# adaLN weight loads moved between the layers of a diffusion backbone step, and the place of one combine in the expert groups

## The reference

```python
mod = (silu(cond) @ ada_w[i] + ada_b[i])            # 1024 -> 6 * 1024, per sequence
sh1, sc1, g1, sh2, sc2, g2 = split(mod, 6)
h = rms_norm(x, norm1_g[i]) * (1 + sc1) + sh1
m = (pool_mix, attention, fourier_mix)[i % 3](h)    # layers 0, 1, 2, 3: pool, attention, fourier, pool
x = x + g1 * m
h = rms_norm(x, norm2_g[i]) * (1 + sc2) + sh2
x = x + g2 * moe(h)                                 # 16 experts of width 512, top 2 in the best group of 4
```

## Time and profile before

| | us |
|---|---|
| median of 3 runs (lowest, highest) | 1356.53 (1354.65, 1357.44) |
| the profiled execution | 1354.35 |
| its span, first to last instruction | 1352.5 |
| TensorE busy | 1267.3 (94%) |
| VectorE busy | 391.5 |
| ScalarE busy | 328.6 |
| read from memory | 532.26 MB, 395 GB/s over the span |

### The profile page before, as it was taken

One profiled execution on the slowest core, in us unless ns is written; L12 is line 12 of the kernel. 1 busy time (PEld: TensorE's weight loads), 2 busy tenths in 40 slices (PEclk: granted clock), 3 DMA queues, 4 the chain that ended last, 5 costly groups with the idle time before them and its releaser, 6 DMA issues.

```text
span 1352.5 us, 18262 instructions
## 1 busy us (share of the span) xinstructions
PE 1267.3 (94%) x6665; PEld 576.3 (43%) x6665; DVE 391.5 (29%) x873; ACT 328.6 (24%) x692; POOL 39.3 (3%) x77
## 2 busy tenths in 40 slices
PE   3877999999999998999999999999999999999996
PEld 0433344343657544443433464443434354434342
DVE  1241222132233314222231413321322443213224
ACT  1231122121322223221221323221212452212122
POOL 3010000000000001000000000000000000000000
PEclk9878999999999999999999999999999999999999
DMA  9999999999997899899999998899999999999995
GB/s 374 419 418 421 420 422 421 423 421 421 343 381 310 324 413 402 340 412 420 421 422 422 418 377 326 339 398 420 422 422 422 415 421 363 405 422 421 421 422 227
DMA packets 87260, 535.21 MB, mean 396 GB/s; under 512 B 11192, under 2 KB 13336, under 8 KB 25760
## 3 DMA queue, kind: packets, MB, share of 16 engines
q1 hardware_dynamic: 82336, 527.47, 95.6%
q0 software_dynamic: 3120, 5.23, 1.2%
q10 hardware_dynamic: 1744, 1.73, 0.4%
HBM read 532.26 MB, written 2.12 MB: 395 GB/s over the span
## 4 chain that ended last, share of the span: by engine, by line
PE 84%; DMA 9%; DVE 4%; ACT 2%; issue 1%; SPq 0%; DVEq 0%; ACTq 0%
PE ps L1869 32%; PE ps L1915 15%; DMA ring<-in_ada_w_dram 5%; PE ps L1855 5%; PE ps L1927 5%; PE ps L1535 4%; PE ps L1499 4%; PE ps L1396 4%; PE ps L1898 3%; PE ps L1544 2%; DMA xh<-in_moe_w_up_dram 2%; DMA ring<-in_attn_wqkv_dram 2%; PE ps L1471 1%; PE ps L1886 1%; PE ps L1705 1%
## 5 line engine op out<-in xcount | busy, mean ns | idle before, releaser
L1869 PE MATMUL ps<-ring,xg 128*64 128x512 f32 x992 | 454.2, 601 | 19.6 <-ACT gu L841 12.3
L1871 PE MATMUL ps<-ring,xg 128*64 128x512 f32 x992 | 451.4, 598 | 0.0
L1869 PEld LDWEIGHTS ps<-ring,xg 128*64 128x64 f32 x992 | 127.6, 137 | 275.2 <-issue 248.2
L1915 PE MATMUL ps<-ring,gb 128*64 128x512 f32 x992 | 225.4, 595 | 0.0
L1319 DVE SCALAR_TENSOR_TENSOR gb<-ps,gslot,g2x 128x512 f32<-128x512 f32 x128 | 90.2, 746 | 257.1 <-PE ps L1915 257.1
L1871 PEld LDWEIGHTS ps<-ring,xg 128*64 128x64 f32 x992 | 126.9, 136 | 0.0
L1915 PEld LDWEIGHTS ps<-ring,gb 128*64 128x64 f32 x992 | 68.4, 137 | 132.2 <-issue 124.6
L854 ACT ACTIVATE y_hi<-gb 128x512 fp32r<-128x512 f32 x128 | 77.1, 626 | 168.3 <-PE ps L1927 108.4
L1396 PE MATMUL ps<-ring,cact 128*32 128x512 f32 x768 | 92.9, 617 | 10.3 <-ACT cact L638 5.3
L841 ACT ACTIVATE gu<-ps 128x512 f32<-128x512 f32 x64 | 38.3, 598 | 231.8 <-PE ps L1871 231.8
L1328 DVE TENSOR_TENSOR y_lo<-gb,y_hi 128x512 fp32r<-128x512 f32 x128 | 83.5, 688 | 12.5 <-ACT y_hi L854 11.9
(11 more groups left out here) (211 smaller groups left out, 1092.8 us busy)
## 6 DMA issues: line engine op xcount, KB each, us to landing
ring<-in_moe_w_up_dram SPq DMA_DIRECT2D x124, 1024.0 KB, 14.8
ring<-in_moe_w_gate_dram SPq DMA_DIRECT2D x124, 1024.0 KB, 13.6
ring<-in_moe_w_down_dram SPq DMA_DIRECT2D x124, 1024.0 KB, 15.4
ring<-in_ada_w_dram SPq DMA_DIRECT2D x96, 1024.0 KB, 17.8
ring<-in_attn_wqkv_dram SPq DMA_DIRECT2D x12, 1024.0 KB, 19.9
spare<-in_moe_w_gate_dram SPq DMA_DIRECT2D x4, 1024.0 KB, 18.8
xh<-in_moe_w_up_dram SPq DMA_DIRECT2D x4, 1024.0 KB, 12.5
hT<-in_moe_w_down_dram SPq DMA_DIRECT2D x4, 1024.0 KB, 13.8
```

The source lines that it names most:

```text
L1869: mg = pe.matmul(ps[0:SLOTS, B_GU, :], xg[:, b, e, :], wg[:, i * F:(i + 1) * F], start=(b == 0), stop=(b == DB - 1))
L1871: mu = pe.matmul(ps[SLOTS:P, B_GU, :], xg[:, b, e, :], wu[:, i * F:(i + 1) * F], start=(b == 0), stop=(b == DB - 1))
L1915: mm = pe.matmul(ps[r * SLOTS:(r + 1) * SLOTS, DOWN_BANKS[e % 2], :], acts[:, e % ACTS, j, :], w[:, i * D + r * HALF:i * D + (r + 1) * HAL ...
```

## The change

Four units of third 3 (of its eight) move from layer 0 to layer 1, and third 10 moves from layer 2 to layer 3.

- Layer 0: the router takes the first four units of third 3 and closes the accumulation there. A new `ada_begun` on VectorE adds this partial sum to the bias rows in place; TensorE waits for it (`s_begun`) before the gathers. The turn and the mods of third 3 leave layer 0.
- Layer 1: units 4 to 7 of third 3 are taken in the fills (one, three, none) and start a new accumulation. `ada_rows(3)` and `ada_mods(3)` stand behind the normed rows on VectorE, `ada_turn(3)` before the fourth part of the transposes. All eight units of third 4 stand where its second four stood.
- Layer 2: third 9 alone; five units in the fills, three behind the projection, its turn behind the second norm's transposes, as third 10's was. Nothing stands behind the sums or between the halves of the projection.
- Layer 3: third 10 in the fills (two, four, two), its rows before and its turn behind the pool matmuls; all eight units of third 11 behind the gates.
- In every expert group the combine of expert 0 stands between `gate_up(2, 1)` and `gate_up(3, 0)`, not before `gate_up(2, 1)`.
- The fourth part of the even norms and of the Fourier sums gets bank `B_ACC + 2`, which is free once x is copied. `keep_busy(14)` and `keep_busy(30)` go.

```diff
@@ -57,16 +57,16 @@
 BEFORE_EXPERTS = [
-    ada_units(0) + [("pool", 0, 0)] + ada_units(1) + ada_units(2) + ada_units(3),
-    ada_units(4)[:4] + matrix_units("qkv", 0) + matrix_units("qkv", 2) + ada_units(4)[4:]
+    ada_units(0) + [("pool", 0, 0)] + ada_units(1) + ada_units(2) + ada_units(3)[:4],
+    ada_units(3)[4:] + matrix_units("qkv", 0) + matrix_units("qkv", 2) + ada_units(4)
     + matrix_units("qkv", 4) + ada_units(5) + matrix_units("qkv", 1) + matrix_units("qkv", 3) + ada_units(6)
     + matrix_units("qkv", 5) + ada_units(7) + matrix_units("wo", 0) + ada_units(8)[:4] + matrix_units("wo", 1) + ada_units(8)[4:],
-    ada_units(9) + matrix_units("four", 0) + ada_units(10)[:4] + matrix_units("four", 1) + ada_units(10)[4:],
-    ada_units(11)[:4] + [("pool", 1, 0)] + ada_units(11)[4:],
+    ada_units(9)[:5] + matrix_units("four", 0) + matrix_units("four", 1) + ada_units(9)[5:],
+    ada_units(10) + [("pool", 1, 0)] + ada_units(11),
 ]
-FILLS = {1: (4, [0, 1, 3, 4]), 2: (9, [0, 1, 3, 3]), 3: (11, [0, 1, 3, 4])}
+FILLS = {1: (3, [4, 5, 8, 8]), 2: (9, [0, 2, 5, 5]), 3: (10, [0, 2, 6, 8])}
@@ -125,7 +125,7 @@
-HT_BANKS = [[0, 1, 2, 0], [B_ACC, B_ACC + 1, B_ACC + 2, B_ACC + 3]]
+HT_BANKS = [[0, 1, 2, B_ACC + 2], [B_ACC, B_ACC + 1, B_ACC + 2, B_ACC + 3]]
@@ -365,6 +365,7 @@
         s_rows = sem("s_rows")
+        s_begun = sem("s_begun")
         s_adat = sem("s_adat")
@@ -461,7 +462,7 @@
-        SUM_BANKS = [0, 1, 2, 0]
+        SUM_BANKS = [0, 1, 2, B_ACC + 2]
         SPECTRUM_BANKS = [(4, 5), (6, 7)]
@@ -986,6 +987,13 @@
+            def ada_begun(t, l, base):
+
+                v.wait_ge(s_used, used(UNIT_AT[("ada", t, 3)], l, base))
+                v.wait_ge(s_adab[t % 2], 64 * (t // 2 + 1))
+                v.tensor_tensor(adabr[:, t % 2, :], ps[:, B_ADA, :], adabr[:, t % 2, :], ALU.add).then_inc(s_begun, 1)
+                v.wait_ge(s_begun, 1)
+
             def ada_mods(t):
@@ -1145,9 +1153,7 @@
-                ada_rows(9, l, bases[l])
                 spectrum(1)
-                ada_mods(9)
                 spectrum(3)
@@ -1245,15 +1251,22 @@
                     normed_rows()
+                    if l == 1:
+                        ada_rows(3, l, base)
+                        ada_mods(3)
                 if KINDS[l] == 2:
...
                 if KINDS[l] == 0:
+                    if l == 3:
+                        ada_rows(10, l, base)
                     mixer_pool(l)
...
                         ada_mods(1)
+                    else:
+                        ada_mods(10)
                     pool_added(l)
@@ -1269,14 +1282,14 @@
                 if l == 2:
-                    ada_rows(10, l, base)
+                    ada_rows(9, l, base)
                 if l == 3:
...
                 if l == 2:
-                    ada_mods(10)
+                    ada_mods(9)
                 router(l)
@@ -1359,8 +1372,7 @@
                 if l == 0:
-                    ada_rows(3, 0, 0)
-                    ada_mods(3)
+                    ada_begun(3, 0, 0)
                 v.wait_ge(s_g2x, 2 * (l + 1))
@@ -1394,7 +1406,7 @@
                         mm = pe.matmul(ps[32 * j:32 * (j + 1), B_ADA, :], cact[:, i, :], w[:, j * 512:(j + 1) * 512],
-                                       start=(i == 0), stop=(i == ADA_UNITS - 1))
+                                       start=(i == 0 or (t, i) == (3, 4)), stop=(i == ADA_UNITS - 1 or (t, i) == (3, 3)))
                     mm.then_inc(s_used, 1)
@@ -1413,14 +1425,17 @@
-            def normed(n):
+            def normed(n, between=None):
...
                         pe.wait_ge(s_xhd, 2 * n + j // 2 + 1)
-                    if n % 2 == 0 and j == 3:
-                        pe.wait_ge(s_ha, 2 * TURNED_BEFORE[n] + 1)
+                    if j == 3:
+                        if between is not None:
+                            between()
+                        if n % 2 == 0 and n > 0:
+                            pe.wait_ge(s_xd, n)
                     for b in (2 * j, 2 * j + 1):
@@ -1601,7 +1616,7 @@
                 turned(K_TURN0, [kT[:, i, 0:SEQ] for i in range(4)])
-                ada(4, 4, ADA_UNITS, l, base)
+                ada(4, 0, ADA_UNITS, l, base)
@@ -1682,7 +1697,7 @@
                     if j == 3:
-                        pe.wait_ge(s_f1a, 1)
+                        pe.wait_ge(s_xd, n)
                     for b in (2 * j, 2 * j + 1):
@@ -1691,10 +1706,12 @@
                 chan = kfour[:, P:P + 1024].rearrange("p (b i n) -> p b i n", b=2, i=2)
-                sums_out(l)
-                ada(9, 3, ADA_UNITS, l, base)
                 for g in range(4):
                     pe.wait_ge(s_f1s, g // 2 + 1)
+                    if g == 0:
+                        sums_out(l)
+                    elif g == 1:
+                        pe.wait_ge(s_f1d, 2)
                     if g == 2:
@@ -1706,8 +1723,6 @@
                     mm.then_inc(s_f2, 1)
-                    if g == 2:
-                        ada_turn(9)
@@ -1725,8 +1740,8 @@
                 pe.wait_ge(s_f3d, 2)
-                project(l, base, "four", [fT[:, b, :] for b in range(DB)], (4, 5, 6, 7), lambda: ada(10, 0, 4, l, base))
-                ada(10, 4, ADA_UNITS, l, base)
+                project(l, base, "four", [fT[:, b, :] for b in range(DB)], (4, 5, 6, 7))
+                ada(9, 5, ADA_UNITS, l, base)
@@ -1776,9 +1791,7 @@
                 if l == 0:
-                    ada(3, 4, ADA_UNITS, l, base)
-                    ada_turn(3)
-                    pe.wait_ge(s_mod, 4)
+                    pe.wait_ge(s_begun, 1)
                 pe.wait_ge(s_tlo, 4 * l + 4)
@@ -1792,7 +1805,7 @@
                 if KINDS[l] != 2:
-                    normed(2 * l)
+                    normed(2 * l, (lambda: ada_turn(3)) if l == 1 else None)
                 if l > 0:
@@ -1810,11 +1823,11 @@
                     else:
+                        ada_turn(10)
                         first_gates(l, 0)
...
                         first_gates(l, 1)
-                        ada(11, 4, ADA_UNITS, l, base)
-                        keep_busy(30)
+                        ada(11, 0, ADA_UNITS, l, base)
                         second_gates(l, 0)
@@ -1826,7 +1839,7 @@
                     normed(2 * l + 1)
-                    ada_turn(10)
+                    ada_turn(9)
                 router(l, base)
@@ -1944,8 +1957,8 @@
                     turn(1)
+                    gate_up(2, 1)
                     combine(0, it8)
-                    gate_up(2, 1)
                     gate_up(3, 0)
@@ -1968,7 +1981,6 @@
                     fill(l + 1, 1, base)
-                    keep_busy(14)
 # ---- launch: one core; inputs and outputs as the reference has them ----
```

## The result

| | before | changed kernel |
|---|---|---|
| median (lowest, highest), 6 runs each | 1356.37 (1354.65, 1357.46) | 1360.82 (1359.05, 1362.27) |
| the profiled execution | 1354.35 | 1362.04 |
| its span | 1352.5 | 1360.2 |

The ratio of the medians is 1.0034, 95% interval 1.0021 to 1.0047: 4.4 us slower, where 1.1 was forecast. The time lies in the stated range (1350 to 1363), above the forecast's own (1355 to 1360), and the likeliest case, a change too small to be told from none, was not the one that came. The same program run again gave 1.0033 (1.0021 to 1.0045) over 12 runs.

What follows compares the result with a forecast made beforehand. Weight loads at 2.49 us each bound the kernel, TensorE where DMA idles. Terms -10.0 + 3.6 + 1.1 - 0.4 - 6.9 + 13.8 - 1.8 + 1.7 = +1.1 us, median 1357.6; range 1350 to 1363.

Steps and rivals of the forecast that it cites:

- the likeliest case: Whole kernel: the time is the same, within about 0.2%, 2.7 us, of no change; chance 0.40.
- Layer 0: Layer 0: four loads fewer at 2.49 us each, TensorE keeping up; -10.0 us, bounds -10.0 to -8.0.
- Layer 1: Layer 1's start: four more loads fill standing DMA, +3.64 us on TensorE, and a longer chain delays the attention, +1.1.
- The start of the attention itself: Layer 1: the chain through norm, transposes and new turn starts the attention +1.1 us later, bounds 0 and +2.5.
- by some 5 us: Sign to watch in layer 1: DMA idle goes down by some 5 us.
- The clock: Layers 1 and 2, before the attention or the Fourier sums: one half-clock loss of 1.7 us in all.
- Layer 2: Layer 2: eight loads fewer, all in standing DMA, so only TensorE's path counts; -6.9 us with the combine, bounds -10 and -3.
- Layer 3: Layer 3: eight loads more, +19.9 us less 6.1 of idle they fill, +13.8, with TensorE ahead; bounds +11 and +15.
- The combine and the end: Combine's new place: -0.4 us each in layers 1 and 2; kernel end: TensorE's lag behind the last landing goes, -1.8.
- Rival 2: Slower: half clock before layer 1's attention and before layer 2's Fourier sums; +5.5 us, 1362; chance 0.18.

Runs made afterwards that it cites:

- the eleven with the half third: Eleven profiles of kernels with four units of third 3 moved to layer 1, the changed kernel's first included; second query projection starts between 410.86 and 412.09.
- the pair: The changed kernel with third 10 left in layer 2, keeping the third 3 move and the combine; 0.9959, 1351.14, and again 0.9968, 1352.10, against before.

## Why the prediction was wrong on the size, step by step

**Layer 0: held, 0.8 short.** -9.2 for -10.0 in this profile, -9.2 to -10.3 in the eleven with the half third, and idle no more than before (3.9 for 4.0 us). TensorE's wait of 7.32 is 1.30 (122.72), the gathers wait for the partial sum and start at 103.16 for the 105.4 foreseen.

```profile
103.16 0.50 PE L1868 MATMUL ps<-onehot,h_hi 128*128 128x256 f32 x2 [3.12 <-DVE adabr L994]
```

**Layer 1: the step that failed.** It read: "The loads fill standing DMA, so +3.64 on TensorE." The idle of the earlier trace rows lies in 395 to 450 and 540 to 580; the four loads come at the layer's start, and the attention takes the qkv loads behind them in order. Room counts only ahead of the first consumer that waits, and there it was some 2 us (2.5 by the rate, 1.8 by the share). At that consumer +7.4 stood for the predicted 1.1 + 3.6 = 4.7. The start of the attention itself was right: +0.9 for +1.1, hidden behind the later wait. The rest of the layer's excess is one half-clock stretch in the router, 0.43 x 4 = 1.7 us, which the next part counts. The stated sign that idle in layer 1 would fall "by some 5 us" was the right one to watch: it fell by 0.3.

**The clock: right in size, short in number, its place not the same in each execution.** One fall of 1.7 us was priced, before the attention or before the sums. Of the falls in the changed kernel's profile two stand where TensorE sets the pace, both in routers:

```profile
343.00:346.00 3.00, 3.00 (x10) 2.41 (x10) 0.00 (x0) 0.65 (x2) 0.79 (x1) 0.61 1.10 371
538.00:542.00 4.00, 4.00 (x16) 2.96 (x15) 3.32 (x16) 0.50 (x1) 0.00 (x0) 0.57 1.02 424
1084.00:1087.00 3.00, 2.48 (x6) 2.06 (x7) 0.12 (x1) 0.00 (x0) 0.00 (x0) 0.56 1.01 421
...
842.00:845.00 3.00, 3.00 (x10) 1.97 (x9) 2.76 (x14) 0.00 (x0) 0.00 (x0) 0.50 0.98 407
```

343 is hidden by the qkv wait, 1084 by layer 3's loads. 538 costs 1.7, 842 costs 0.50 x 3 = 1.5; together 3.2 for the 1.7 in the sum. Before the sums the clock stayed at 1.00 in this profile in spite of three loads with waits between (764.41, 766.90, 769.40: 0.28, 1.42, 1.44 us), where the forecast half expected a fall. It was not wrong to: with third 10 alone, behind waits of 1.43 and 1.46 us at the same place, the clock fell for twice as long:

```profile
771.00:778.00 7.00, 5.93 (x27) 4.27 (x28) 0.33 (x2) 1.68 (x5) 0.00 (x0) 0.52 1.05 387
```

Of the six profiles of kernels with third 10 in layer 3, three fell there (third 10 alone, and both with transposes in layer 3: 0.57 over 768 to 772 and over 771 to 775) and the other three fell in layer 2's router. From the layer's start the spectrum began 18.7 us on in the three without the fall at the sums, and 20.2, 20.3 and 21.6 in the three with it.

**Layer 2: held but for the clock.** The fifth load's four matmuls ended with the sums starting at 770.40, x was copied, and the spectrum began at 775.60 (foreseen 776.1, less the layer's shift of 0.6, is 775.5). The second norm's transposes began at 829.74, 7.1 earlier than in the earlier trace rows, 6.5 of it within layer 2; the sum had -6.5 up to there and -0.4 for the combine. The fall at 842 took 1.5 back. Idle grew by 14.1 us for 13.

```profile
769.40 1.06 PE L1408 MATMUL ps<-ring,cact 128*32 128x512 f32 x8 [1.44 <-DMA ring<-in_ada_w_dram]
770.40 3.84 PE L1704 MATMUL ps<-kfour,xh 128*128 128x128 f32 x32
775.60 1.10 PE L1722 MATMUL ps<-kfour,fsum 128*128 128x256 f32 x4 [1.36 <-issue]
...
829.74 1.97 PE L1442 MATMUL ps<-const,xh 128*128 128x128 f32 x16 [1.73 <-ACT xh L653]
```

**Layer 3: right in mechanism, 1.5 too small.** 8 x 2.49 = 19.9 less the idle filled. I took 6.1; by the ledger 7.7 became 3.4, so 4.3 was filled, which gives 15.6 for the 15.3 measured. The first group is full, as foreseen; what idle is left stands elsewhere (1.0 us of it at the end: 333 GB/s over 1338 to 1343). Against the earlier trace rows, and without the 5.9 that layer 3 began earlier, the pooling started 7.8 later (7.4 foreseen) and the second gates, at 1107.73, 10.5 later (9 foreseen), both under the 15.3 of the loads, as the step needed. TensorE waits for single loads all through the start:

```profile
1071.62 1.07 PE L1408 MATMUL ps<-ring,cact 128*32 128x512 f32 x8 [1.44 <-DMA ring<-in_ada_w_dram]
1074.10 1.93 PE L1408 MATMUL ps<-ring,cact 128*32 128x512 f32 x8 [1.41 <-DMA ring<-in_ada_w_dram]
...
1084.52 2.05 PE L1486 MATMUL ps<-ring,hT 128*128 128x256 f32 x4 [1.88 <-DMA ring<-in_pool_w_dram]
```

**The combine and the end: right together, wrongly split.** The tail lost 1.7 us. The combine alone takes it, and third 10 alone takes it too (layer 3's loads landed 12.1 later, the span was 10.4 longer), so it belongs to neither and is had once, as the sum had it.

The misses against the profile add up: layer 0 +0.8, layer 1 at the qkv wait +2.7, the clock +1.5, layer 3 +1.5, small ones +0.1, 6.6 in all. Some 3 us of that is the pair of profiles, not the kernels: between medians the miss is 3.3. Rival 2's total (+5.5) is nearer to the median, but its mechanism is borne out in part at most: the fall before the attention costs nothing, and the one before the sums came in some executions and not in this one. That the whole came within the range is owed to layers 0, 2 and 3, whose terms held within 1.6 us each; layer 1's, the largest miss, was not foreseen by any rival.

The Trainium skill, "TensorE: Matmul & The Clock Gate", section "HAM oscillation — how this bites in real kernels", has matmul bursts between DMA waits fall to half clock each time; the waits of its own example are of 3 to 5 us, and those here are shorter. At these it was not each time: in the changed kernel's profile there was a fall behind the waits of 1.4 us in layer 3 (at 1074) and none in layer 2, where waits of 1.42 and 1.44 us left 765 to 800 at 1.00, and with third 10 alone there was one in layer 2 as well.

## What to carry to other kernels

Idle of the transfer engines is room for a moved load only if it lies between the load's new place and the first consumer behind it in the same ordered stream that already arrives just in time: compute that consumer's landing, not the layer's total of idle, and tell time in which the engines stand from time in which they are slow. Here four loads moved to a head that was full cost three quarters of their transfer time, with some 25 us of idle further on; so test each half of a move by itself. And once such a wait stands, time that TensorE saves ahead of it is worth nothing.

## What the runs showed of the hardware that was not expected

- **Where the clock falls varies between executions of the same program.** In the changed kernel's second profile there was none at the attention's start, though the wait ahead of it was the same 2.99 us; instead one followed a wait of 3.80 us for the qkv load:

```profile
342.00:346.00 4.00, 4.00 (x20) 3.54 (x19) 0.00 (x0) 0.54 (x2) 0.70 (x1) 1.00 1.07 310
411.00:414.00 3.00, 2.36 (x6) 1.95 (x7) 0.00 (x0) 0.00 (x0) 0.00 (x0) 0.60 1.03 418
841.00:845.00 4.00, 4.00 (x12) 2.49 (x12) 3.65 (x18) 0.00 (x0) 0.00 (x0) 0.59 0.98 410
```

- In the pair's profile the attention's start fell (0.59 over 342 to 346) and the projection behind its qkv wait of 1.71 us did not (1.00 over 411 to 414). So one profile's count of falls can't be carried to another by the waits alone, and a price for the clock is good to about one fall, 1.5 to 1.7 us.
- The router of layer 2 fell in both profiles of the changed kernel, behind waits of 1.73, 1.59 and 0.81 us, and not in that of before, where the wait for ScalarE's xh was 0.86. The longer wait is not what it takes: both profiles of the pair fell in the same router behind a wait for xh of 0.87 us (0.63 over 846 to 850 and 0.57 over 849 to 853).

Open: whether the attention could take its qkv loads singly, or whether the four units of third 3 could stand behind them, was not tried; either would say how much of the 7.4 us can be had back.
